# C's attention moved ahead of A and B, into one block with the value rows and the first units; five projection units run inside it as half units

## What is computed

```
for l in range(DEPTH):
    h = rms_norm(x, norm_mix_pre[l])
    ua, ub, uc, ud = jnp.split(h @ w_in[l], SPLITS, axis=-1)
    oa = rms_norm(gqa_axial(ua, ...), g_out_a[l])
    ob = rms_norm(mla(ub, ...), g_out_b[l])
    oc = diff_attention(uc, ..., g_out_c[l], slopes, lambda_init)
    od = rms_norm(neighbourhood_attention(ud, ...), g_out_d[l])
    x = x + rms_norm(jnp.concatenate([oa, ob, oc, od], -1) @ w_out[l], norm_mix_post[l])
    f = jnp.square(jax.nn.relu(rms_norm(x, norm_mlp_pre[l]) @ w_up[l])) @ w_down[l]
    x = x + rms_norm(f, norm_mlp_post[l])
# diff_attention, per head and block of queries:
    sc = q @ k.T * scale - slope * |distance|      # two maps, m = 0, 1
    p = softmax(sc);  a = p[0] - lam * p[1];  o = a @ v
```

## Time and profile before

| | us |
|---|---|
| median of 3 runs | 2885.76 (2885.73 to 2887.87) |
| the profiled execution | 2882.37 |
| its span | 2880.6 |
| PE busy, whole span | 2686.5 (93%) |
| VectorE, ScalarE, GpSimd busy | 1889.2, 1360.5, 531.1 |
| layer 0: projection; A and B; C; D | to 273; to 485; to 622; to 680 |
| layer 1: projection; A and B; C; D | from 1460; from 1692; from 1915; from 2052 |

### The profile page before, as it was taken

How to read it: one execution, slowest core, us unless ns; L and a number is a source line. 1 busy time by engine, 2 the same in 40 slices (tenths; PEclk the granted TensorE clock), 3 DMA queues, 4 the chain that set the end, 5 groups by cost and what they waited for, 6 DMA issues and landing times. The chain is left out here.

```text
span 2880.6 us, 36563 instructions
## 1 busy us (share of the span) xinstructions
PE 2686.5 (93%) x13768; PEld 2249.1 (78%) x13768; DVE 1889.2 (66%) x2756; ACT 1360.5 (47%) x2344; POOL 531.1 (18%) x479
## 2 busy tenths in 40 slices
PE   7998998987979999999989999989879899999998
PEld 5887997676858887888869879967767688878887
DVE  6514876976688876445773158769766877764456
ACT  4313776975443332433433147669754432334342
POOL 2211534960000000000022224449400000000000
PEclk9999998998989999999989999989989899999999
DMA  6544675452224445766523456854322344467665
GB/s 179 137 135 131 199 213 154 65 147 62 71 90 156 151 146 189 263 212 199 189 70 105 132 151 181 239 137 69 116 67 75 102 148 161 146 208 236 217 203 161
DMA packets 332970, 433.00 MB, mean 150 GB/s; under 512 B 86134, under 2 KB 211834, under 8 KB 332540
## 3 DMA queue, kind: packets, MB, share of 16 engines
q1 hardware_dynamic: 331932, 429.10, 49.4%
q10 hardware_dynamic: 864, 1.57, 0.2%
HBM read 288.00 MB, written 140.86 MB: 149 GB/s over the span
## 5 line engine op out<-in xcount | busy, mean ns | idle before, releaser
L2352 PE MATMUL f_ps<-dn_g 128*128 128x512 f32 x2688 | 614.6, 390 | 10.4 <-DVE dn_g L2589 10.4
L2352 PEld LDWEIGHTS f_ps<-dn_g 128*128 128x128 f32 x2688 | 504.8, 188 | 118.2 <-DVE dn_g L2589 8.2
L2589 DVE TENSOR_TENSOR dn_g<-dn_raw,dn_g 128x2048 fp32r<-128x2048 f32 x112 | 256.5, 2291 | 256.0 <-ACT dn_g L2434 255.8
L2434 ACT ACTIVATE dn_g<-dn_raw 128x2048 fp32r<-128x2048 f32 x112 | 214.6, 1916 | 354.4 <-PE f_ps L2352 279.8
L2342 PE MATMUL f_ps<-hc_h,up_w_h 128*128 128x512 f32 x896 | 352.4, 393 | 25.2 <-DVE up_w_l L2555 18.8
L2342 PE MATMUL f_ps<-hc_h,up_w_l 128*128 128x512 f32 x896 | 351.5, 392 | 0.0
L2342 PEld LDWEIGHTS f_ps<-hc_h,up_w_h 128*128 128x128 f32 x896 | 170.2, 190 | 62.6 <-DVE up_w_l L2555 26.7
L1204 DVE TENSOR_REDUCE nmax_ab<-s_ps_ab 128x1 f32<-128x1024 f32 x128 | 156.7, 1224 | 94.4 <-PE s_ps_ab L1091 94.3
L2342 PE MATMUL f_ps<-hc_ld,up_w_h 128*128 128x512 f32 x512 | 200.8, 392 | 0.0
L2342 PEld LDWEIGHTS f_ps<-hc_h,up_w_l 128*128 128x128 f32 x896 | 170.0, 190 | 35.6
L1158 ACT ACTIVATE pt_h_ab<-t_ps_ab 128x512 fp32r<-128x512 f32 x256 | 139.5, 596 | 87.5 <-PE t_ps_ab L197 87.2
(11 more groups left out here) (301 smaller groups left out, 5985.1 us busy)
## 6 DMA issues: line engine op xcount, KB each, us to landing
act_blocks<-u_stage SPq DMA_DIRECT2D x32, 1792.0 KB, 6.6
dn_raw<-act_blocks SPq DMA_DIRECT2D x112, 512.0 KB, 4.0
mix<-in_w_down SPq DMA_DIRECT2D x128, 256.0 KB, 3.9
down_sums<-mix SPq DMA_DIRECT2D x128, 256.0 KB, 2.9
up_raw<-in_w_up SPq DMA_DIRECT2D x32, 1024.0 KB, 5.6
dn_raw<-down_sums SPq DMA_DIRECT2D x64, 512.0 KB, 5.1
dn_raw<-in_w_down SPq DMA_DIRECT2D x48, 512.0 KB, 4.9
w_raw<-in_w_in SPq DMA_DIRECT2D x16, 512.0 KB, 4.3
```

Source lines behind the costliest of these rows:

```text
L2352: last = nc.tensor.matmul(f_ps[:, bank0[pi] + i, :], lhs[:, n % 4, 0, q, i * P:(i + 1) * P], rhs[:, n % 4, 1, q, :], start=(down_opens[pi] ...
L2434: nc.scalar.activation(g_h[:, n % 4], dn_raw[:, n % 3], ACT.Copy).then_inc(S["d_hi"], 1)
L2589: nc.vector.tensor_tensor(g_l[:, n % 4], dn_raw[:, n % 3], g_h[:, n % 4], ALU.subtract) \
```

## The change

`projection_stage` and `difference_stage` are gone. In their place stand `front_stage` (value rows, units 0 to 2, C's attention for all four heads, units 3 to 7 as ten half units in it, and the first six rows of A's weights) and `rows_stage` (A's rows, B's rows, B's rope, keys, queries and values). A and B follow as before; D's q and k, its bias tables and the mask work are now loaded and done beside A and B; C's result goes through HBM (`c_mix`) and is put into `mix` at the end of A and B. C's heads are loaded one at a time, into two places. The MLP's tail works on half widths. The opening loads the value columns of six weight rows in place of A's.

The core of the diff (the new blocks are cut to what decides their order):

```
+                def fill_part(n):
+
+                    i = 1 if n == 1 else n // 4 + 1 if n >= 4 and n % 4 == 0 else FILLS
+                    return (i, 0, 3 * KT) if i < FILLS else None
+
+                def fill_taken(n):
+
+                    i = 1 if n == 2 else n // 4 + 1 if n >= 5 and n % 4 == 1 else FILLS
+                    return i if i < FILLS else None
...
+                    def load_head(h):
+                        units = 2 * (h // 2) + 2
+                        for j in range(2):
+                            sp.wait_ge(S[f"spilled{j}"], 32 * units)
+                            sp.wait_ge(S[f"v_spilled{j}"], 16 * (NT // 2))
...
+                        if h >= 2:
+                            sp.wait_ge(S["pv_done"], NT // 2 * (h - 1))
...
+                    unit(3)
+                    spill_unit(0)
+                    unit(4)
+                    spill_unit(1)
+                    load_head(0)
+                    load_head(1)
+                    unit(5)
+                    spill_unit(2)
+                    spill_fill(0)
+                    unit(6)
+                    spill_fill(1)
+                    unit(7)
+                    spill_fill(2)
+                    load_head(2)
+                    spill_mix(0)
...
+                    sp.wait_ge(S["max_done"], 2 * N_ALL)
+                    sp.wait_ge(S["fill_done"], 8)
+                    for r in range(A_FIRST):
+                        sp.dma_start(a_source(r), w[r * P:(r + 1) * P, A0:A0 + 8 * HD]).then_inc(S[f"a_row_landed{r // 2}"], 16)
+                    spill_fill(8)
+                    spill_fill(9)
+                    spill_mix(3)
...
+                    def fill(i, lo, hi):
+
+                        u = LEAD + i // 2
+                        if lo == 0:
+                            pe.wait_ge(S["w_lo"], u + 1)
+                            if i >= 1:
+                                pe.wait_ge(S["fill_lo"], i)
+                        for at in range(lo, hi):
+                            k, j = at // 3, at % 3
+                            wt, x_ = ((u_h, h_hi), (u_h, h_lo), (u_l, h_hi))[j]
+                            last = nc.tensor.matmul(fill_ps, wt[u % 3][:, k, :], x_[:, k, half(i)], start=(at == 0),
+                                                    stop=(at == 3 * KT - 1))
...
+                    scores(0, 0)
+                    scores(0, 1)
+                    fill(0, 0, 3 * KT)
+                    for n in range(N_ALL + VALUE_LAG + 1):
+                        if n + 1 < N_ALL:
+                            scores(n + 1, 0)
+                        if 0 <= n - TURN_LAG < N_ALL:
+                            turn(n - TURN_LAG, 0)
+                            turn(n - TURN_LAG, 1)
+                        if n + 1 < N_ALL:
+                            scores(n + 1, 1)
+                        s = n - VALUE_LAG
+                        if s >= 1 and s % 2 == 0:
+                            finish(s // 2 - 1)
+                        if fill_part(n) is not None:
+                            fill(*fill_part(n))
+                        if 0 <= s < N_ALL:
+                            values(s // 2, s % 2)
...
+                    def fill_high(i):
+                        u = LEAD + i // 2
+                        act.wait_ge(S["fill_done"], i + 1)
+                        act.wait_ge(S[f"spilled{i % 2}"], 32 * u)
+                        nc.scalar.activation(st_h[:, half(i)], fill_ps, ACT.Copy, scale=unit_scale(u)) \
+                            .then_inc(S["fill_hi"], 1)
...
+                    exponential(0, 0)
+                    exponential(0, 1)
+                    scale_sum(0)
+                    fill_high(0)
+                    for n in range(N_ALL + VALUE_LAG):
+                        if fill_taken(n) is not None:
+                            fill_high(fill_taken(n))
...
+                        if n == N_ALL + 1:
+                            a_row_high(0)
+                        if n == N_ALL + 2:
+                            for r in range(1, A_FIRST):
+                                a_row_high(r)
...
+                    maximum(0, 0)
+                    maximum(0, 1)
+                    fill_low(0)
+                    for n in range(N_ALL + VALUE_LAG + 1):
+                        if n + 1 < N_ALL:
+                            maximum(n + 1, 0)
+                        if fill_taken(n) is not None:
+                            fill_low(fill_taken(n))
+                        if n < N_ALL:
+                            weigh(n)
+                        if n + 1 < N_ALL:
+                            maximum(n + 1, 1)
```

The end of `rows_stage` (PE, then VectorE), and what is loaded beside A and B:

```
+                    pe.wait_ge(S["bw_lo"], 3)
+                    pe.wait_ge(S["back_lo"], 2 * NT)
+                    query_unit(2, t_ps[:, 0, :])
+                    query_unit(3, t_ps[:, 1, :]).then_inc(S["rope_gemm"], 1)
+                    pe.wait_ge(S["row_taken"], 2 * NT)
+                    for j in range(2):
                         key_unit(j, unit_out(j)).then_inc(S["kv_gemm"], 1)
                     pe.wait_ge(S["rope_done"], 1)
...
+                    for e in range(NHEAD):
+                        key_low(e)
+                    rope()
+                    rope_low()
...
+            def fetch_d(sp):
                 sp.wait_ge(S["scores_done"], N_MAPS_A * NT)
+                sp.wait_ge(S["pv_done"], N_MAPS_A * NT // 2)
...
+            def fetch_ab(sp):
+                fetch_sums(sp, sum_steps, {SUMS_IN_A: fetch_d, SUMS_IN_A + 10: fetch_biases})
+                for h in range(NHEAD):
+                    sp.dma_start(mix[:, :, (8 + h) * HD:(9 + h) * HD], c_mix[h]).then_inc(S["c_landed"], 16)
...
+            def pool_in_ab(pool):
+                make_sums(pool, sum_steps)
+                mask_bias(pool)
```

The MLP's tail, per far tile k:

```
+                    def far_norm(k):
+                        s = HT + k
+                        after(nc.vector.tensor_tensor(far_y[:, :], c_far[:, k, NEAR], g_post[:, NEAR], ALU.mult))
...
+                        for y, part in ((far_y[:, :], NEAR), (c_far[:, k, FAR], FAR)):
+                            nc.vector.scalar_tensor_tensor(out=x[:, part], in0=y, scalar=stat[:, 0, s:s + 1], in1=x[:, part],
+                                                           op0=ALU.mult, op1=ALU.add).then_inc(S["far_added"], 1)
```

More of the change, by code:

```diff
@@ L300, in projection_stage @@
[L300 to L315, removed]
+                row_col = (A0, B0)
+                row_width = (NA, NB)
+                row_dst = ((w1_h, w1_l), (w2_h, w2_l))
+                N_ROWS = 2 * KT - A_FIRST
+                def row_of(q):
+                    r = q + A_FIRST
+                    return r // KT, r % KT
@@ L340, in unit @@
[L340 to L350, removed]
@@ L417, in _, with row @@
-                    sp.wait_ge(S["row_lo"], 3 * KT)
+                    def row(q):
+                        part, k = row_of(q)
+                        if q >= 2:
+                            sp.wait_ge(S["row_lo"], q - 1)
+                        sp.dma_start(row_source(q), w[k * P:(k + 1) * P, row_col[part]:row_col[part] + row_width[part]]) \
+                            .then_inc(S[f"row_landed{q % 2}"], 16)
+                    for q in range(2):
+                        row(q)
+                    for dst, name in ((gc_q, "cos_a"), (gs_q, "sin_a")):
+                        sp.dma_start(dst[:, :, :], a[name].rearrange("(t p) d -> p t d", p=P)).then_inc(S["const_landed"], 16)
@@ L418, in _ @@
+                    for q in range(2, N_ROWS):
+                        row(q)
+                    sp.wait_ge(S["row_lo"], N_ROWS)
                     for k, rows in enumerate(w_rows[0:2]):
@@ L443, in _ @@
                                          a["cos_sin_b"][j * B_ROPE:(j + 1) * B_ROPE, :]).then_inc(S["table_landed"], 16)
[L444 to L448 removed]
+                    sp.wait_ge(S["row_done"], 2 * NT)
+                    sp.wait_ge(S["back_lo"], 2 * NT)
                     for dst, part in ((B["k_h"], b_h), (B["k_l"], b_l)):
@@ L457, in _ @@
                                 .then_inc(S["stack_landed"], 16)
-                    for j in range(2):
-                        sp.wait_ge(S[f"spilled{j}"], 2 * 16 * 4)
                     sp.wait_ge(S["stack_landed"], 16 * (2 + 2 * NHEAD))
@@ L493, in _, with row_low @@
-                    if opening:
-                        set_constants()
-                    for r in range(3 * KT):
-                        row_low(r)
-                    unit_weight_low(0)
-                    unit_weight_low(1)
+                    clear_last(pool)
+                    def row_low(q):
+                        part, k = row_of(q)
+                        hi, lo = row_dst[part]
+                        pool.wait_ge(S["row_hi"], q + 1)
+                        nc.gpsimd.tensor_tensor(lo[:, k, :], row_source(q), hi[:, k, :], ALU.subtract).then_inc(S["row_lo"], 1)
@@ L499, in _ @@
+                    for q in range(N_ROWS):
+                        row_low(q)
```

(7 more changed lines are left out.)

1344 lines of the change are left out of this document (693 added, 651 removed).

## The result

The changed kernel takes 3002.99 us (median of 4 runs, 3001.20 to 3003.97), the kernel before 2886.48 in the same comparison: a ratio of 1.0402, 95% interval 1.0384 to 1.0420. It is slower, as forecast, by 116.5 us where I had 96. The profiled execution took 3001.2 us, its span 2999.4, against 2880.6.

What follows compares the result with a forecast made beforehand. PE was taken to bound attention A, B and the projection's units, VectorE to bound C. Terms summed to +48.1 us a layer, +96 in all: 2982 us on the median's scale (2978 profiled), range 2925 to 3012.

Steps and rivals of the forecast that it cites:

- Units: Projection: five units of 10.88 us each leave it, all on the path, -54.4 us a layer.
- Hand-over: Between unit 2 and C: PE idles until head 0 is reloaded from spills, +10 us a layer, range 8 to 23.
- Start of C: C's first tiles: a copy waits for unit 2's spill behind head 1's loads, +19 us a layer, range 7 to 24.
- Seven half units: C's tiles 4 to 28: each half unit leaves VectorE idle, 5.5 us each, +38.5 us a layer, range 19 to 43.
- End of C: C's drain: the last half unit, then DMA or GpSimd's weight splits end last, +6 us a layer, range 2 to 10.
- B's head work: Rows stage: normed rows, transposes and rope lose their cover, so PE idles, +15 us a layer, range 8 to 20.
- End of A and B: D's later loads, twelve bias loads and GpSimd's masks outlast the stage, +14 us a layer, range 0 to 20.
- MLP tail: Last MLP tiles: half-wide steps multiply and add at once, -2 us a layer, range -4 to 0.
- (1): Every stage: PE's work sets its length, so the kernel gets faster, 2852 us; chance 0.07.
- (2): C: VectorE's gap after a fill is half recovered, seven fills cost 19 us, total 2943; chance 0.15.
- (3): A and B: their end stays hidden as the sums close up, total 2954 us; chance 0.14.
- (4): C: heads 2 and 3 land 6 to 12 us late each, total 3006 to 3030 us; chance 0.08.

Runs made afterwards that it cites:

- e8: Changed kernel with unit 3 ahead of C, eight half units quartered, unit 2's spill and loads of D, heads 2, 3 moved, rope first: 2859.79 us, ratio 0.9926.
- e3: Changed kernel with unit 2's spill and the load of unit 5's weights both issued ahead of head 1's loads: 2981.55 us, ratio 1.0344.
- e11: Changed kernel with only the load of unit 5's weights issued ahead of head 1's loads: 2994.41 us, ratio 1.0391.
- e12: Changed kernel with only the spill of unit 2 issued ahead of head 1's loads: 3006.73 us, ratio 1.0434.
- e4: Changed kernel with 21 of the 24 products left out of each of the seven steady half units of a layer: 2945.60 us, ratio 1.0216.
- e2b: Changed kernel with half units 1 to 9 cut into thirds, each placed between the fold and the values: 2986.54 us, ratio 1.0358.
- e6: Changed kernel with B's rope and its high half ahead of the four key halves instead of behind them: 2988.02 us, ratio 1.0363.
- e5: Kernel before with only the changed kernel's MLP tail: 2880.91 us, ratio 0.9994.
- e1: Changed kernel with D's q and k loaded ahead of step 24 instead of 17, bias edges ahead of 28 instead of 27: 2964.58 us, ratio 1.0287.
- the thirds kernels: Changed kernel with half units 1 to 9 cut into thirds, placed behind the values (2993.33 us) or ahead of them (2986.54 us).

## Why the prediction was right, and where it was off

- *Units*, -54.4 a layer: the products of the units are 226.7 ns apart in the new places too; right.
- *Hand-over*, +10: PE idle 10.43 and 9.50 us, ended by head 0's v, which has the last of the nine loads. Right, and by its own steps: head 0 was there 21.3 us after unit 1 (forecast 20.9). e8 puts unit 3 there: its first scores are at 121.97, hardly later than the changed kernel's 121.61.
- *Start of C*, +19: +15.3 up to the sixth maximum, 12.7 of it at the second tile (forecast 15). The principle held (a small transfer behind 2.6 MB); the step that named the instruction was wrong. It let ScalarE wait at the half unit's copy for the spill. It waited first for unit 5's weights, in program order ahead of the exponentials, and the spill was second by 2 us (e3, e11, e12). That the number came near all the same is in part luck: another transfer, which I had counted only as data ahead of the spill, landed 1 to 2 us ahead of it.
- *Seven half units*, 5.5 each: the gap of VectorE is 4.72 us (forecast 4.8), and four tiles take 21.05 (forecast 20.1). The 0.9 that is missing is the wait for the bank, a cost of the half unit's place in PSUM that I did not look for (e4, e2b). With it a half unit cost 6.45 us, above the 6.1 of my upper end, which was to be the case that nothing is hidden. Over the stretch from the sixth to the last maximum it came to +41.2 for +38.5, since three slower tiles of before (4.49 in place of 3.65 us) are in the comparison.
- *End of C*, +6: +6.9. C as a whole came to +63.9 and +64.4 for a forecast of +63.5. That this is so near is luck: the start was 3.7 too large, the half units and the end 3.6 too small.
- *B's head work*, +15, and the cold start, +2: together 19.5 and 21.7. The wait for the rope is 8.40 (forecast 8.5), that ahead of the last transposes and products 2.60 + 1.26 (forecast 4.3 less 0.5). That the order on VectorE made the rope's part, e6 showed. The remaining 2.5 and 4.7 us I did not take apart. The low clock is the likely part of it: I had 2.7 us for it, and the 24 query products alone lost 3.6, besides the head products, whose granted clock was 0.65.
- *End of A and B*, +14: +21.5 and +19.9. This is the step that was mis-sized. D's loads began 14.7 us later in the stage than C's had (105.3 against 90.6; forecast 15). The sums ended 35.7 us later (forecast 31): GpSimd stood still for 21.0 us over the twelve bias loads, whose issue I had at 17 (it was 17.26). Masks 8.5 (8). And the next stage came 1.9 us behind the last mask, which I had at 0. These three misses, 4.7, 0.5 and 1.9 us, are the difference in layer 0. What made the chain so long was neither of these but SP's 29.2 us of standing at step 17; the forecast had it within the later start, and took the place of the loads as given.
- *MLP tail*, -2 a layer: +0.9 and -4.0 for the whole MLP. The sum is near the forecast, the shape is not: the gain is in the last MLP alone (e5).
- *Rivals*. (1), PE's work as the length of every stage, is out for this kernel and became nearly true for e8, with all four corrections (17.95 us for 17.3). (2), half of the gap recovered, is out: nothing was. (3), a hidden end of A and B, is out here and is what e1 makes. (4), late heads 2 and 3: no such wait is in the changed kernel; the thirds kernels had one of its kind, behind head 3's loads.

The lower end of my range was generous (my lower ends add up to -14 a layer, not -13), and its upper end was near: 3003 lies 21 us above my 2982 and 9 below 3012. Of the terms that missed by more than 0.5 us in layer 0, the start of C and D's stage (-1.3 for 0) came out cheaper than forecast; the half units, the end of C, the rows stage, the end of A and B, the MLP and the opening (2.2 us for 0) came out dearer.

## What to carry to other kernels

Filler work for TensorE inside a stage that another engine bounds cost less the smaller its pieces were: a lump of 5.44 us cost 6.45, more than outside the stage, the same work in thirds 4.2 and in quarters 3.35. My reading, which no run bounds, is that a piece should be no longer than TensorE's own slack plus what the buffers ahead of the bound engine hold (0.65 + 0.6 us here, and a quarter is 1.36). Look also at what the filler takes beside time, here a PSUM bank whose loss made a wait of 1.23 us. In a queue that runs in order, ask of every issue who waits for what stands behind it, and let a wait of the queue come at the point of its work list where it would wait least; moving two such points and one order on VectorE was worth 33, 17 and 11 us.

## What was not expected of the hardware

An issue of SP can itself be held up: one spill's issue behind head 1's loads took 7.06 us (0.32 to 0.47 us in other places), and the load of the weights ahead of it 6.59. Both stand behind 5.2 MB of loads; that the length of an issue shows how full the queue is, is my reading, which no run tests. Runs of one kernel spread further on the four chips of the experiments than in the first comparison (e6 and e8 15 us, the kernel before 4 to 7, there 2), so the ratios with their intervals carry the small differences.
